# First attention's stream reordered, x's squares added by pairs, and two-column token sums in the MLPs

## What is computed

```python
mod = (c_act @ ada_w[layer] + ada_b[layer])[:, None, :]
sh_a, sc_a, gt_a, sh_m, sc_m, gt_m = jnp.split(mod, 6, axis=-1)
h = modulate(rms_norm(x, attn_norm[layer]), sh_a, sc_a)
...
a = p[:, :, 0] - lam_full * p[:, :, 1]
...
x = x + gt_m * squared_relu_mlp(h, mlp_w1[layer], mlp_w2[layer])
...
return rms_norm(x, final_norm)
```

## Time and profile before

| what | value |
|---|---|
| median of three runs | 2426.03 us |
| profiled execution, time | 2426.29 us |
| profiled execution, span | 2424.5 us |
| TensorE busy | 2290.5 us, 94% |
| VectorE busy | 1206.0 us, 50% |
| ScalarE busy | 509.0 us, 21% |
| mean granted TensorE clock | 0.972 |

### The profile page before, as it was taken

The page is one execution under the profiler, slowest core; times in us unless marked ns, Lnnn a source line. Parts: engine busy times, 40 slices in busy tenths (PEclk is TensorE's granted clock), DMA queues, the critical chain, the costliest instruction groups (busy, mean ns, idle before and its releaser), DMA issues. The chain is left out here.

```text
span 2424.5 us, 26465 instructions
## 1 busy us (share of the span) xinstructions
PE 2290.5 (94%) x9806; PEld 1522.8 (63%) x9806; DVE 1206.0 (50%) x2762; ACT 509.0 (21%) x1149; POOL 43.0 (2%) x50
## 2 busy tenths in 40 slices
PE   7999899999999999989999999999999998889886
PEld 4444586888887655558688888844578443333332
DVE  4444575667776256666455666567566111111014
ACT  2233212330002144441233100112232000000001
POOL 0000000000000000000000000000000000000000
PEclk9999999999999999999999999899998999999999
DMA  7544313353532211103444444311033679999995
GB/s 298 222 161 175 116 70 138 140 208 139 208 140 113 70 53 53 61 35 139 180 167 181 166 181 167 139 70 70 1 139 141 227 328 427 426 427 426 423 424 220
DMA packets 45459, 452.73 MB, mean 187 GB/s; under 512 B 7784, under 2 KB 7784, under 8 KB 20240
## 3 DMA queue, kind: packets, MB, share of 16 engines
q1 hardware_dynamic: 37616, 435.64, 45.0%
q0 software_dynamic: 6528, 12.17, 1.4%
q10 hardware_dynamic: 1184, 3.19, 0.3%
HBM read 444.54 MB, written 18.39 MB: 191 GB/s over the span
## 5 line engine op out<-in xcount | busy, mean ns | idle before, releaser
L2996 PE MATMUL ps<-ring,big 128*64 128x512 f32 (+1 forms) x768 | 233.5, 611 | 28.1 <-issue 15.9
L1193 PE MATMUL ps<-big,ring 128*128 128x256 f32 x768 | 185.8, 379 | 0.6 <-PE ps L1111 0.6
L2996 PEld LDWEIGHTS ps<-ring,big 128*64 128x64 f32 (+1 forms) x768 | 85.4, 151 | 146.9 <-issue 133.8
L3092 DVE TENSOR_TENSOR big<-big,ps 128x512 f32<-128x512 f32 x20 | 13.8, 688 | 295.5 <-ACT big L3061 281.4
L537 PE MATMUL ps<-hT,ring 128*128 128x512 f32 x336 | 153.7, 607 | 5.9 <-DMA ring<-in_stream 5.9
L1193 PEld LDWEIGHTS ps<-big,ring 128*128 128x128 f32 x768 | 145.8, 190 | 21.1 <-issue 1.4
L1111 PE MATMUL ps<-hT,ring 128*128 128x256 f32 x672 | 154.3, 379 | 1.5 <-ACT big L1260 1.5
L2077 PE MATMUL ps<-hT,ring 128*128 128x512 f32 x320 | 144.1, 606 | 2.8 <-DVE big L2459 1.7
L1111 PEld LDWEIGHTS ps<-hT,ring 128*128 128x128 f32 x672 | 127.5, 190 | 20.3 <-issue 3.1
L1025 DVE SCALAR_TENSOR_TENSOR ring<-ring,tmp 128x1024 f32<-128x1024 f32 x112 | 136.1, 1219 | 0.0
L2996 PE MATMUL ps<-big 128*64 128x512 f32 (+1 forms) x352 | 128.9, 600 | 7.1 <-ACT big L3057 3.3
(11 more groups left out here) (509 smaller groups left out, 3664.2 us busy)
## 6 DMA issues: line engine op xcount, KB each, us to landing
ring<-in_stream SPq DMA_DIRECT2D x99, 2048.0 KB, 8.5
ring<-in_gate SPq DMA_DIRECT2D x17, 2048.0 KB, 29.7
ring<-in_up SPq DMA_DIRECT2D x16, 2048.0 KB, 25.8
ring<-in_down SPq DMA_DIRECT2D x15, 2048.0 KB, 28.6
big<-in_up SPq DMA_DIRECT2D x9, 2048.0 KB, 25.5
big<-in_down SPq DMA_DIRECT2D x8, 2048.0 KB, 27.6
big<-in_gate SPq DMA_DIRECT2D x7, 2048.0 KB, 24.3
hT<-in_down SPq DMA_DIRECT2D x5, 2048.0 KB, 27.1
```

Source lines behind the costliest of these rows:

```text
L1193: ins = pe.matmul(m.ps[:, bank[name], q * H:(q + 1) * H], a[:, q * P:(q + 1) * P], b, start=(first and q == 0), stop=(final and q == 1))
L2996: ins = pe.matmul(out[a:z, :], left[:, k * P + a:k * P + z], bufs[i % WBUF][:, k * width + c * 512:k * width + (c + 1) * 512], start=(k == ...
L3092: dve.tensor_tensor(hid[:, s, :], hid[:, s, :], m.ps[:, 3 + 2 * s, :], ALU.mult).then_inc(hid_ok, 1)
```

## The change

The stream of the first attention is reordered, by one written order used by the loader's array and by the phase. The second head's weights come one place sooner. The first and the last head have no modulation chunk; heads 3 and 5 (counted from 0) have two, the others one. At the start VectorE adds x's squares by pairs, and TensorE sums four tiles in place of eight. In the MLPs the accumulated squares are summed at step 24 of the second product, each sum is a matmul with two columns of factors (1 and the squared gain), and the squares of tiles 4 to 7 are summed once for both norms; the weighted squares of these tiles are no longer made.

```diff
                 dve.tensor_copy(rb[:, 0:512], m.ps[0:16, 0, :]).then_inc(bias_sb, 3)
+                for k in range(0, KT, 2):
+                    dve.wait_ge(sqd, k + 2)
+                    dve.tensor_tensor(m.hT[:, k, :], m.hT[:, k, :], m.hT[:, k + 1, :], ALU.add).then_inc(paired, 1)
                 dve.wait_ge(cond_ok, 1)
...
                 pe.wait_ge(m.go, 3)
-                for k in range(KT):
-                    pe.wait_ge(sqd, k + 1)
+                for k in range(0, KT, 2):
+                    pe.wait_ge(paired, k // 2 + 1)
                     for j in range(NT):
                         last = pe.matmul(m.ps[:, 3 + j, 0:1], m.hT[:, k, j * P:(j + 1) * P], m.ones[:, 0:1],
-                                         start=(k == 0), stop=(k == KT - 1))
+                                         start=(k == 0), stop=(k == KT - 2))
                 last.then_inc(summed, 1)
...
     return m.big[:, 7424:7424 + 2048].rearrange("p (s m n) -> p s m n", s=2, m=2)
+MOD_HEAD = {4: 1, 5: 2, 6: 3, 7: 3, 8: 4, 9: 5, 10: 5, 11: 6}
+def diff_order():
+    order = [("head", 0), ("mod", 2), ("mod", 3), ("head", 1)]
+    for h in range(1, DIFF_HEADS - 1):
+        order += [("mod", c) for c in sorted(MOD_HEAD) if MOD_HEAD[c] == h] + [("head", h + 1)]
+    return order
+DIFF_ORDER = diff_order()
...
-            return at if h == 0 else at + 2 + 2 * h
-        def modulations(h):
-            return at + 3 + 2 * h
+            return at + DIFF_ORDER.index(("head", h))
+        def taken(h):
+            return [c for c in range(4, 12) if MOD_HEAD[c] == h]
...
-                    n = at + c - 1
+                    n = at + DIFF_ORDER.index(("mod", c))
                     dve.wait_ge(m.full[n % RING], 16 * (n // RING + 1))
...
-                def modulate(h, j):
-                    n = modulations(h)
+                def modulate(c, j):
+                    n = at + DIFF_ORDER.index(("mod", c))
                     if j == 0:
                         dve.wait_ge(m.full[n % RING], 16 * (n // RING + 1))
-                    o = 16 + 4 * h + j
+                    o = 4 * c + j
                     modulation_tile(m, dve, n, j, crow, m.mod0[:, o:o + 1]).then_inc(mod_done, 1)
                     if j == 3:
-                        dve.wait_ge(mod_done, 8 + 4 * (h + 1))
+                        dve.wait_ge(mod_done, 4 * (c - 1))
                         dve.sem_inc(m.free[n % RING], 1)
...
                 for h in range(heads):
+                    own = [(c, j) for c in taken(h) for j in range(4)]
                     for j in range(4):
                         bias(h, 3 - j)
-                        modulate(h, j)
+                        for c, tile in own[j * len(own) // 4:(j + 1) * len(own) // 4]:
+                            modulate(c, tile)
                     dve.wait_ge(expd, 8 * h + 8)
...
     cres = m.rs[:]
-    inner2 = m.tmp[:, 1024:1032]
+    factors = m.tmp[:, 1024:1040].rearrange("p (f c) -> p f c", c=2)
+    either = m.tmp[:, 1040:1044].rearrange("p (f c) -> p f c", c=2)
+    sums_at = m.ps[:, 7, 0:2 * NT].rearrange("p (i c) -> p c i", c=2)
...
+                def token_sums(sq, factor, start, stop):
+                    for i in range(NT):
+                        ins = pe.matmul(m.ps[:, 7, 2 * i:2 * i + 2], sq[:, i * P:(i + 1) * P], factor,
+                                        start=(start and i == 0), stop=(stop and i == NT - 1))
+                    return ins
                 def products(s, names):
...
                     products(s, ["P6", "P5", "P7", "P2", "P4", "P3"])
+                    if s == 24:
+                        pe.wait_ge(freed, 3)
+                        if inner is None:
+                            token_sums(sq1.acc, m.ones[:, 0:2], True, False)
+                        else:
+                            pe.wait_ge(freed2, 3)
+                            pe.wait_ge(weighed, 1)
+                            token_sums(sq1.acc, either[:, 0, :], True, False)
+                            token_sums(sq2.acc, either[:, 1, :], False, False)
                 for name in ("P1", "P6", "P5", "P7", "P2", "P4", "P3"):
...
-                def token_sums(out, sq, start, stop):
-                    for i in range(NT):
-                        ins = pe.matmul(out[:, i:i + 1], sq[:, i * P:(i + 1) * P], m.ones[:, 0:1],
-                                        start=(start and i == 0), stop=(stop and i == NT - 1))
-                    return ins
-                pe.wait_ge(v4_ok, 2)
-                pe.wait_ge(freed, 3)
-                token_sums(m.ps[:, 1, 0:NT], sq1.acc, True, False)
-                if inner is not None:
-                    pe.wait_ge(c22_ok, 2)
-                    pe.wait_ge(freed2, 3)
-                    token_sums(m.ps[:, 2, 0:NT], sq2.acc, True, False)
                 released(7)
-                keep_busy(m, pe, 7, 4)
+                pe.wait_ge(v1_ok, 2)
+                keep_busy(m, pe, 0, 4)
                 for j in range(4, 8):
                     pe.wait_ge(sqd, j + 1)
-                    token_sums(m.ps[:, 1, 0:NT], sq1.at(j), False, j == 7).then_inc(summed, 1)
-                    if inner is not None:
-                        pe.wait_ge(sqd2, j + 1)
-                        token_sums(m.ps[:, 2, 0:NT], sq2.at(j), False, j == 7).then_inc(summed2, 1)
-                keep_busy(m, pe, 7, 3)
+                    token_sums(sq1.at(j), m.ones[:, 0:2] if inner is None else factors[:, order[j], :], False, j == 7
+                               ).then_inc(summed, 1)
+                keep_busy(m, pe, 0, 3)
                 pe.wait_ge(inverse, 1)
...
                             act.wait_ge(summed, j - 5)
-                        if inner is not None and j < 6:
+                        if inner is not None and j < 4:
                             square_rows(m, act, sq2, inner, j, freed2, sqd2, order[j])
...
                     act.wait_ge(summed, 4)
-                    act.activation(m.st[:, 0:NT], m.ps[:, 1, 0:NT], ACT.Sqrt, bias=m.eps[:, 0:1], scale=1.0 / D).then_inc(rooted, 1)
+                    act.activation(m.st[:, 0:NT], sums_at[:, 0, :], ACT.Sqrt, bias=m.eps[:, 0:1], scale=1.0 / D).then_inc(rooted, 1)
                 else:
...
                     act.activation(m.st[:, 0:NT], m.st[:, 0:NT], ACT.Sqrt, bias=m.eps2[:], scale=1.0 / D).then_inc(rooted, 1)
-                    act.activation(m.st[:, NT:2 * NT], m.ps[:, 1, 0:NT], ACT.Sqrt, bias=m.eps[:, 0:1], scale=1.0 / D
+                    act.activation(m.st[:, NT:2 * NT], m.st[:, NT:2 * NT], ACT.Sqrt, bias=m.eps[:, 0:1], scale=1.0 / D
                                    ).then_inc(rooted, 1)
...
                     dve.wait_ge(c11, len(pairs))
-                    c2.link(dve.tensor_tensor(inner2, inner, inner, ALU.mult))
+                    c2.link(dve.memset(factors[:, :, 0], 1.0))
+                    c2.link(dve.memset(either, 0.0))
+                    for j in range(2):
+                        c2.link(dve.memset(either[:, j, j:j + 1], 1.0))
+                    dve.tensor_tensor(factors[:, :, 1], inner, inner, ALU.mult).then_inc(weighed, 1)
                 sums(0)
...
                 outputs(1)
-                if inner is not None:
-                    for j in (6, 7):
-                        f = order[j]
-                        dve.wait_ge(summed2, j - 5)
-                        dve.scalar_tensor_tensor(sq2.at(j), m.xT[:, f, :], inner2[:, f:f + 1], m.xT[:, f, :], ALU.mult, ALU.mult
-                                                 ).then_inc(sqd2, 1)
                 o, z = 0, 16 * tiles
...
                     dve.wait_ge(summed, 4)
-                    dve.wait_ge(summed2, 4)
-                    c2.link(dve.tensor_scalar(m.st[:, 0:NT], m.ps[:, 1, 0:NT], EPS, None, ALU.mult))
-                    dve.tensor_tensor(m.st[:, 0:NT], m.st[:, 0:NT], m.ps[:, 2, 0:NT], ALU.add).then_inc(whole, 1)
+                    c2.link(dve.tensor_copy(m.st[:, NT:2 * NT], sums_at[:, 0, :]))
+                    dve.scalar_tensor_tensor(m.st[:, 0:NT], m.st[:, NT:2 * NT], EPS, sums_at[:, 1, :], ALU.mult, ALU.add
+                                             ).then_inc(whole, 1)
                 dve.wait_ge(rooted, 1)
...
     ada2 = output_rows(I["ada_w_2"][0], 384)
-    parts = [ada0[:2], heads[:1], ada0[2:4], interleave(ada0[4:11], heads[1:]), ada0[11:], chunks(I["a_w_out"][0]),
+    parts = [ada0[:2], np.stack([(heads if kind == "head" else ada0)[j] for kind, j in DIFF_ORDER]), chunks(I["a_w_out"][0]),
              interleave(chunks(I["mlp_w1"][0]), ada1[:8]), interleave(mlp_down(I["mlp_w2"][0]), ada1[8:])]
```

More of the change, by code:

```diff
@@ L238, in phase_start @@
         sem = ph.sem
-        small, consts, xin, sig, chn, cond_in, cond_ok, mod_done, bias_mm, bias_sb, lamc, sqd, summed, rooted, inverse = (
+        small, consts, xin, sig, chn, cond_in, cond_ok, mod_done, bias_mm, bias_sb, lamc, sqd, paired, summed, rooted, inverse = (
```

(6 more changed lines are left out.)

## The result

The changed kernel took 2411.96 us (median of 5 runs, 2409.92 to 2414.21), the kernel before 2424.86 us beside it: a ratio of 0.9946, 95% interval 0.9931 to 0.9960. Run three times more, it gave 0.9931 [0.9919, 0.9944], 0.9935 [0.9921, 0.9950] and 0.9930 [0.9911, 0.9947]. It is faster, by 13 to 17 us, where 21 were forecast. The profiled execution spans 2410.2 us at a mean granted clock of 0.969.

What follows compares the result with a forecast made beforehand. TensorE, busy 94% of the span, was taken to bound the kernel. Gains of 4.9 (start), 8.0 (second head's weights), 1.5 (last head), 6.7 (second MLP) and 0 sum to 21.1 us, giving 2404.9 us, range 2400.5 to 2410.0.

Steps and rivals of the forecast that it cites:

- the last head: Last attention head: four modulation tiles leave VectorE, so the reciprocal comes sooner; gain 1.5 us, between 1.2 and 4.8.
- The walk through scores, bias and exponentials: Last head, step by step: last scores start at 276.0 not 276.50, reciprocal at 277.9 not 279.4.
- Second MLP: End of the second MLP: sums shortened, spreading at 1553.4 not 1560.58; 7.2 less 0.5 for clock, 6.7 us, range 3.5 to 8.
- First MLP: End of the first MLP: 8 records move forward, 32 stay; taken as nothing, range 2 us worse to 1 better.
- Behind the first MLP: Stages after it: they start when earlier ones end, so nothing at a fixed time eats the gain; no cost.
- Start and second head's weights: Start: pair additions bring the reciprocal 4.9 us sooner; first attention: second head's weight wait and low clock go, 8.0 us.
- The 0.8 us to spare: First projection: seventh input tile wanted at 49.2, given at 48.4 by the last chunk; costed at nothing.
- rival 1: Clock gives back at the MLPs' ends: second MLP 4.0, first 2 worse, total 16.4, 2409.6 us; chance 0.15.
- Rival 5: First attention: second head's weights still wait on a slot freed late; gain 13.1, 2412.9 us; chance 0.03.
- Late weights: Rival 4: fifth, seventh and eighth heads' weights land after TensorE asks; 2432.8 us with 20 us transfers; chance 0.02.
- rivals 2 and 3: 2: start bound by transfers, 2406.9 us, chance 0.15; 3: last head gives 3.5, first MLP 1, 2401.9 us, chance 0.1.

Runs made afterwards that it cites:

- two variants: Changed kernel plus last-head filling matmuls (3, 16, 4 and 4), 2402.69 us; same with 14 in the large place and seventh head's sums behind the last scores, 2402.72 us.
- the third: Changed kernel plus last-head filling matmuls, 9 before the combined weights, and the seventh head's sums of squares behind the last scores: 2404.52 us, 0.9914.
- the plain fills: Changed kernel plus filling matmuls in the last head: 3 before second scores, 16 before combined weights, 4 before and 4 after head sums; 2402.69 us, 0.9907.

## Why the prediction was wrong

**The step that failed is the last head,** "1.5 us, between 1.2 and 4.8", where every bound was a gain. The walk through scores, bias and exponentials was right: in the four profiles without the tiles whose first low stretch lies as before (10.2 us, from 6.3 to 7.1 us after the head's first scores; 6.4 in the kernel before) the transposes come 1.4 to 1.5 us sooner. In the three others that stretch starts 4.2 to 4.8 us after the first scores and lasts 13.7 us, and the transposes are hardly sooner or not at all, at 13.06 to 13.35 us. What the walk left out is TensorE's clock behind the wait. Without the tiles the clock falls a second time, just under the spreading, which takes 6.5 to 6.8 us in all seven profiles; with them it does so in two of seven, for 3.4 us and not 6.8, and the spreading takes 3.8 in five and 5.4 in those two. Last head and out projection cost 2.9 us in place of giving 1.5. That is 4.4 of the 5.8 us between the forecast's 21.1 and the stages' 15.3. That one chunk's move is enough is shown by the stages of the kernel before with that edit alone, where last head and out projection are 2.1 and 2.3 us longer, and that it is the clock by the windows and the fills. The totals alone would not show it.

**Second MLP,** 6.7 forecast, 5.7 measured. A two-column record among the products takes 0.115 us, the bound that I took, and the 1.8 us at step 24 came as reckoned. I had the last sums done 5.1 us after the last product (1551.8 - 1546.7); they ended 6.0 after it (1543.16 + 4.89 - 1542.05). So up to the mixer it gave 6.4 us and not 7.2, and the mixer, for whose start at the lower clock I had taken off 0.5, grew by 0.7.

**First MLP,** forecast 0, measured 0.5 worse, within the 2 us that I had kept. Most of it is where the eight records move forward: 0.9 more in the products, 0.5 less behind them. The 0.9 us more from the filling matmuls to the compression is regained in the compression.

**Behind the first MLP,** forecast 0. "The later stages start when the earlier end, so nothing stands at a fixed time to eat it" took the sparse attention as unchanged; it is 2.9 us longer in the mean with the MLPs' edit, at a lower granted clock. The kernel with the MLPs' edit alone has it, the two with the pair additions or the stream alone have not. One profile of the kernel before has it too and one of the changed kernel has not, so it is a matter of how often, and what in the edit brings it is not shown.

**Start and second head's weights** were right: 5.1 against 4.9, 7.9 against 8.0, with 32 records ending at 22.7 against 22.5, additions of 0.69 us, and 3.70 us for the second head's first eight. For the first modulation chunk of the ring I had two arrivals, 33.6 and, with the tables taking all that they need, 36.1; VectorE waited 2.37 us and had it at 34.35, nearer to the first. The 0.4 us that I gave the semaphore after a landing no row shows; here that chunk landed at 34.33 and was used at 34.35. The 0.8 us to spare held: the first projection's 48 records took 23.79 us against 23.28 in rows 2, but without a gap; seven of them are slow ones of 0.86 us where the kernel before has six, and the other ten profiles with the pair additions take 22.33 to 23.18. The Trainium skill (DMA: Bandwidth & Descriptors, section "Queues, rings and completion order", on arbitration) has each DMA engine take turns between queues packet by packet. Read as equal shares, which it does not say, that asked for the first head's weights at 31.2. They landed at 28.8, with the tables' copies under way since 22.8, against 28.7 with no delay at all; so the trace does not agree with equal shares here.

**Rivals.** The clock did give back, as in rival 1, whose 2409.6 is close to the medians of the three later sets (2408.17 to 2409.94); that is partly luck, since its places were wrong. It had 2.7 us lost at the second MLP and 2 at the first, where 1.0 and 0.5 were; the loss was in the last head, and in the sparse attention between the MLPs. Rival 5's 2412.9 is nearest to the first set's 2411.96 by number alone: the second head's weights did not wait. Late weights, the rival on the slower side, did not occur: the group of L555 has no idle time. Neither did rivals 2 and 3.

**What stays open.** The table's stages give 15.3 us, and 12.4 with the sparse attention; the three later sets of runs give 16 to 17, and the first set 12.9 with an interval of 9.7 to 16.7. From the mixer to the end, where the kernels have the same instructions, the profiles lie between 851.4 and 860.0 us, so a few us of a total can be owed to that. Why executions of one kernel prefer one length or another there stays open. So does the reason why the clock falls again after the rise in the last head; the profiles show that it does so without the tiles and not with the fills in their place, and what TensorE did in between.

**A better version.** The changed kernel with fills in the last head, 2402.7 us by two variants (0.9907 and 0.9903; 0.9914 and 2404.52 by the third), is faster than the kernel before, and by the medians of the two faster than the changed kernel by 5 to 9 us. The two kernels were not run side by side: the intervals of the plain fills, [0.9893, 0.9920], and of the changed kernel, [0.9931, 0.9960] to [0.9911, 0.9947], are apart in two of the four sets and touch or overlap in the others.

## What to carry to other kernels

Taking work off the engine that TensorE waits for can cost time: read in the windows whether TensorE stands near a change of its granted clock there, and what short, costly group of matmuls lies behind it. Where a stretch becomes sparse, price the group behind it at the low clock too, as a loss, and try filling matmuls with the removal. Cut several profiles at the same records before believing a difference of a few us in a total, and cut the stages that the edit does not touch as well: here one of them took back 2.9 us.

## What was not expected of the hardware

- A stretch near full clock between two at about 0.51 lasted only 3.4 us in the last head, in all seven profiles without the tiles.
- Sixty-four one-column records without a gap left the clock low: 0.215 us each, and 0.218 for the 32 that remained; sums of the same kind in the second MLP ran at 0.115. The profile of the kernel before has no clock on record ahead of 40.9 us, so the 1.00 in the first window of the earlier trace rows is no reading. Its third profile has 0.50 from 14.8 to 38.7 us, and so has the changed kernel's second, here with its 32 records:

```profile
15.50:23.00 7.50, 6.96 (x32) 6.90 (x32) 6.20 (x11) 4.04 (x7) 0.00 (x0) 0.50 1.01 429
```

- Two-column float32 sums cost what one-column sums cost: 16 in 1.84 us in both kernels.
- Two executions of one kernel differ by 11 us of 2420, in stages where the windows show different granted clocks (1.00 against 0.84, 0.96 against 0.87).
